# Two chained two-layer blocks on one core: conv entry of the second layer and both attention entries, in another order of work

## The chip, the cores and the metric

One core of one Trainium2 chip runs the whole program. The metric is device time in microseconds (us) of that core, the median of several runs. TensorE (PE in the rows), VectorE (DVE), ScalarE (ACT), GpSimd (POOL) and SyncE (SP, here only a DMA queue and its waits) each run an instruction stream that was written out by hand, and they meet only at semaphores.

## What is computed

Two different blocks of two layers each, on a sequence of 512 tokens with 1024 channels. Everything below happens in the first block, in which a layer is:

```
ml = ada_mod(c, w_ada[l], b_ada[l], 6); mc = ada_mod(c_ctx, ...)
zl = modulate(x, ml[0], ml[1]) @ w_in[l] + b_in[l]          # 512 tokens
q, k, v = qkv_heads(zl); context k, v from ctx (256 tokens) # 8 query heads, 2 key heads
attn = softmax(q @ k_all.T * scale) @ v_all                 # 768 keys
conv = silu(layer_norm(depthwise_conv(a * sigmoid(gt), 31 taps))) @ conv_pw_w
pool = multiscale_pool(...) @ pool_w
x = layer_norm(ALPHA * x + ml[2] * ((g0*attn + g1*conv + g2*pool) @ w_out))
x = layer_norm(ALPHA * x + ml[5] * conv_ffn(modulate(x, ml[3], ml[4])))
```

The first layer (l = 0) treats 768 tokens, latent and context together, the second (l = 1) 512 tokens, and of the context only keys and values. Between the layers a small projection for the second block ("ple") is computed early and stored.

## The kernel before

**Weights.** A unit is a 128x1024 block of fp32 weights, the columns for one output tile of 128 channels. SyncE loads it into one of two raw buffers (w_raw, by the parity of the unit), ScalarE rounds it into w_hi (weight_hi, L1398), VectorE or GpSimd subtracts to get w_lo (L2188 on VectorE in the conv stages, L550 on GpSimd in the attention and behind it). w_hi and w_lo have four slots. A product takes 24 matmuls for a unit: w_hi with act_hi, w_lo with act_hi, w_hi with act_lo, eight chunks each. ScalarE "refills" a slot (refill) after it has taken the result of the unit that used it, and SyncE loads a raw buffer when the subtraction that read it is done. So unit 7 can't be loaded before unit 5 is split, and SyncE's list is in order: a wait in it holds all loads behind it.

**Conv entry of the second layer.** The stage "conv" has 16 units: even ones give the values, odd ones the gates. Units 0 to 3 run together (first_four, L633), so that TensorE can follow the input chunk by chunk. Then single units (L684) follow. ScalarE takes an even unit with Identity (L1590), an odd one with Sigmoid (L1593), each followed by a refill. Behind the first of them stand the two copies of the "ple" projection out of PSUM tiles 3 and 2 (L1599) and the DMA that stores it (L1602). VectorE multiplies a pair to a chunk (glu, L2388), subtracts a weight half, does some taps of the 31-tap depthwise convolution (conv_taps: a tap is one instruction, L2411 or L2419 in turn; a chunk ends with an addition L2425 and begins with a copy L2401), subtracts the next half, and so on. Ahead of certain units TensorE does a step of the modulation matrices (ada_ahead, ada_step, L872), whose weights SyncE loads between the units and only once an earlier step has freed their buffer. ADA_AT says ahead of which unit stands which step. Step 24 is the first one that sums into PSUM tile 2, so it waits until the second "ple" copy has left that tile:

```python
                    if h == 24:
                        pe.wait_ge(tile_free[2], taken(l, "ada_rest", 2, 0))
```

**Attention.** The 32 tiles of 128 queries go in order (attention, three functions of this name for TensorE, ScalarE and VectorE). For tile it: TensorE makes the scores (s_tile, L987 or L993), VectorE the maximum (L2362, L2364), ScalarE exp (L1519), VectorE the normalization (L2369, L2371), TensorE the transposes (t_tile, L788), ScalarE copies them out (L1529), TensorE multiplies with the values (pair, L800). TensorE's order is scores of it + 2, transposes of it, half a pair. Scores of it + 2 wait for exp of it, transposes for the normalization. VectorE's order is normalization of it, maximum of it + 2, conv taps (more_taps: per_tile, 1 in the first layer, 2 in the second). Before the first tile ScalarE takes the value tiles (L1654) in two copies. In the second layer it then makes the w_hi of two units (L1398), which GpSimd splits, and loads the table for exp (L1673). TAPS_AT holds how many taps stand where, its last number those in front of the merge of the third gate (at_first_unit).

## Time and profile before

| | |
|---|---|
| median of 3 runs | 3144.55 us (3144.37 to 3147.13) |
| profiled execution: time, span | 3145.95 us, 3144.2 us |
| TensorE busy | 3064.6 us, 97% |
| VectorE, ScalarE, GpSimd busy | 63%, 37%, 26% |
| conv stage of the second layer, by the trace | about 1456.9 to 1563 us |
| attention of first and second layer | about 374 to 483 and 1697 to 1817 us |

A row of a timeline has the start (us from the start of the span), the duration, the engine, the line of the kernel, the operation, what it writes and reads, the shape and how many instructions of one form were merged. In brackets stands how long the engine had been idle before it and what ended that. The chain shows which engine's work led to the end: TensorE's has 89% of it.

### The profile page before, as it was taken

To read this page: it belongs to the slowest core of one execution; us is meant where nothing else is said; L and a number is where in the kernel's file an instruction comes from. 1 tells how busy PE (TensorE), PEld (TensorE's weight loads), DVE (VectorE), ACT (ScalarE), POOL (GpSimd) and SP (SyncE) were. 2 spreads that over 40 slices of the span, in tenths; PEclk is the share of its full clock that TensorE was granted. 3 is DMA by queue.
4 is the path that set the end of the run, shared out by engine and by line. 5 is a ranking of instruction groups with operands and counts; after the bars stand their busy time and mean duration, and the time that the engine had idled before them with its cause. 6 is when DMAs were issued, how large, how long until landed. Compare 5 with 4: busy or idle time off the path is not lost.

```text
span 3144.2 us, 43692 instructions
## 1 busy us (share of the span) xinstructions
PE 3064.6 (97%) x16056; PEld 2598.6 (83%) x16056; DVE 1979.9 (63%) x2784; ACT 1152.7 (37%) x1661; POOL 806.7 (26%) x330
## 2 busy tenths in 40 slices
PE   7999999999999999999999999999999999999998
PEld 5999887899999999997777677778887686777766
DVE  5899987644576164356989985664646466445443
ACT  3122364233243221224334535443223535443443
POOL 0001212233323232231012024511545332233312
PEclk8999999999999999999999999999999999999999
DMA  7442001112212212123541022423233212122212
GB/s 289 175 171 82 28 1 65 45 59 101 81 61 67 73 60 67 61 67 136 193 163 55 1 67 87 144 80 101 94 95 108 75 59 79 54 78 77 78 60 67
DMA packets 77709, 275.25 MB, mean 88 GB/s; under 512 B 8688, under 2 KB 11888, under 8 KB 76656
## 3 DMA queue, kind: packets, MB, share of 16 engines
q1 hardware_dynamic: 70800, 253.94, 24.3%
q10 hardware_dynamic: 6752, 19.14, 1.7%
q8 instruction: 108, 1.77, 0.2%
q14 instruction: 49, 0.40, 0.0%
HBM read 266.75 MB, written 6.29 MB: 87 GB/s over the span
## 4 chain that ended last, share of the span: by engine, by line
PE 89%; DVE 5%; ACT 2%; issue 1%; DVEq 1%; DMA 0%; SPq 0%; ACTq 0%
PE ps L684 53%; PE ps L1065 11%; PE ps L619 5%; PE ps L633 2%; PE ps L800 2%; PE ps L1210 1%; PE ps L872 1%; PE ps L963 1%; PE ps L788 1%; PE ps L993 1%; PE ps L1289 1%; DVE small L2362 1%; PE ps L691 1%; PE ps L1307 1%; PE ps L1016 1%
## 5 line engine op out<-in xcount | busy, mean ns | idle before, releaser
L550 POOL TENSOR_TENSOR w_lo<-w_raw,w_hi 128x1024 fp32r<-128x1024 f32 x308 | 789.8, 2568 | 2195.9 <-ACT w_hi L1398 2195.9
L1398 ACT ACTIVATE w_hi<-w_raw 128x1024 fp32r<-128x1024 f32 x376 | 395.8, 1056 | 561.5 <-PE ps L684 286.6
L684 PE MATMUL ps<-act_hi,w_hi 128*128 128x384 f32 (+1 forms) x2544 | 529.8, 356 | 4.4 <-DVE w_lo L2188 2.5
L684 PE MATMUL ps<-act_hi,w_lo 128*128 128x384 f32 (+1 forms) x2544 | 519.4, 352 | 0.0
L684 PE MATMUL ps<-act_lo,w_hi 128*128 128x384 f32 (+1 forms) x2544 | 519.2, 352 | 0.0
L684 PEld LDWEIGHTS ps<-act_hi,w_hi 128*128 128x128 f32 x2544 | 451.0, 188 | 70.5 <-issue 34.7
L684 PEld LDWEIGHTS ps<-act_hi,w_lo 128*128 128x128 f32 x2544 | 455.0, 188 | 32.4
L684 PEld LDWEIGHTS ps<-act_lo,w_hi 128*128 128x128 f32 x2544 | 454.3, 188 | 32.3 <-issue 0.5
L2256 DVE SCALAR_TENSOR_TENSOR x<-ps,mod,x 128x384 f32<-128x384 f32 (+1 forms) x128 | 64.2, 546 | 277.3 <-PE ps L684 222.7
L2419 DVE SCALAR_TENSOR_TENSOR x<-arena,vec,x 128x512 f32<-128x512 f32 x336 | 228.2, 706 | 0.0
L2411 DVE SCALAR_TENSOR_TENSOR arena<-arena,vec 128x783 f32<-128x783 f32 (+1 forms) x240 | 226.2, 943 | 0.0
L2658 DVE SCALAR_TENSOR_TENSOR arena<-arena,vec 128x769 f32<-128x769 f32 (+1 forms) x88 | 145.9, 1658 | 15.4 <-issue 15.4
L1471 ACT ACTIVATE arena<-ps,vec 128x768 f32<-128x768 f32 (+3 forms) x64 | 50.8, 794 | 277.4 <-PE ps L684 206.7
L1065 PE MATMUL ps<-act_hi,w_hi 128*128 128x512 f32 x432 | 117.5, 403 | 1.9 <-ACT vec L1440 0.8
L1065 PE MATMUL ps<-act_lo,w_hi 128*128 128x512 f32 x432 | 111.7, 390 | 1.5 <-DVE act_lo L2734 1.5
L1065 PE MATMUL ps<-act_hi,w_lo 128*128 128x512 f32 x432 | 111.5, 390 | 0.0
L2655 DVE TENSOR_SCALAR arena<-arena,vec 128x769 f32<-128x769 f32 (+1 forms) x44 | 29.1, 661 | 125.7 <-ACT arena L1796 125.7
L1796 ACT ACTIVATE arena<-ps 128x384 f32<-128x384 f32 (+3 forms) x88 | 33.8, 440 | 202.1 <-PE ps L684 197.1
L800 PE MATMUL ps<-arena 128*128 128x256 f32 x416 | 103.1, 381 | 2.6 <-ACT arena L1663 2.5
L2162 DVE TENSOR_TENSOR ffn_lo<-arena,ffn_hi 128x768 f32 (+1 forms) x44 | 101.1, 2298 | 6.5
L1065 PEld LDWEIGHTS ps<-act_hi,w_hi 128*128 128x128 f32 x432 | 78.7, 188 | 28.2 <-issue 12.1
L1065 PEld LDWEIGHTS ps<-act_lo,w_hi 128*128 128x128 f32 x432 | 80.8, 188 | 19.9 <-DVE act_lo L2734 3.3
(380 smaller groups left out, 4551.8 us busy)
## 6 DMA issues: line engine op xcount, KB each, us to landing
w_raw<-in_weights SPq DMA_DIRECT2D x376, 512.0 KB, 3.4
arena<-in_ada_w SPq DMA_DIRECT2D x75, 512.0 KB, 4.8
tmp<-in_ada_w SPq DMA_DIRECT2D x21, 512.0 KB, 6.3
x<-in_x SPq DMA_DIRECT2D x2, 1536.0 KB, 19.2
x<-in_x ACTq DMA_DIRECT2D x1, 3072.0 KB, 10.5
arena<-in_pool_w ACTq DMA_DIRECT2D x2, 1024.0 KB, 4.8
x_mid<-x ACTq DMA_DIRECT2D x1, 2048.0 KB, 7.1
x<-x_mid ACTq DMA_DIRECT2D x1, 2048.0 KB, 8.4
```

Of the source, the lines that this page charges most:

```text
L550: nc.gpsimd.tensor_tensor(WL[:, w], raw, WH[:, w].bitcast(f32), ALU.subtract).then_inc(units_split, 1)
L619: last = nc.tensor.matmul(ps(tb + s, o, o + b - a), w[:, s * UNIT + k * P:s * UNIT + (k + 1) * P], act[:, k * TOK + a:k * TOK + b], start= ...
L633: last = nc.tensor.matmul(tile(0, s, o, o + b - a), w[:, s * UNIT + k * P:s * UNIT + (k + 1) * P], act[:, k * TOK + a:k * TOK + b], start= ...
L684: last = nc.tensor.matmul(tile(o, o + b - a), w[:, s * UNIT + k * P:s * UNIT + (k + 1) * P], act[:, k * TOK + a:k * TOK + b], start=(n == ...
L800: last = nc.tensor.matmul(ps(3, (m % 2) * 512, (m % 2) * 512 + 2 * P), values(m, k), AR[:, a:a + 2 * P], start=(k == 0), stop=(k == nk - 1))
L1065: return nc.tensor.matmul(out, w0[:, k0:k0 + P], act[:, k * n:k * n + SEQ], start=start, stop=stop)
L1398: nc.scalar.activation(WH[:, s * UNIT:(s + 1) * UNIT], RAW[:, (s % 2) * UNIT:(s % 2 + 1) * UNIT], ACT.Copy).then_inc(hi_done, 1)
L2162: return V.tensor_tensor(lo, src, hi.bitcast(f32), ALU.subtract)
L2256: last = V.scalar_tensor_tensor(x, ps(t, o, o + b - a), at(MOD, mod(l, gate, j, m), 1), x, ALU.mult, ALU.add)
L2411: t = V.scalar_tensor_tensor(acc, src, w, acc, ALU.mult, ALU.add)
L2419: t = V.scalar_tensor_tensor(acc, src, w, acc, ALU.mult, ALU.add)
L2658: t = V.scalar_tensor_tensor(cv, src, w, cv, ALU.mult, ALU.add)
```

## The change

It moves work and adds or removes none, apart from where taps of the convolution are done. (1) Second layer, conv entry: the two "ple" copies and their store stand behind ScalarE's fourth unit and no longer behind its first. (2) The modulation steps 24 to 31 stand ahead of units 5, 7, 9, 11, 13, 15, 16, 17 instead of 3, 5, ..., 17. (3) Both attention entries: the table for exp is loaded ahead of the copies of the value tiles. (4) Second layer: the two weight halves that ScalarE made there come behind tiles 4 and 8. (5) Both layers: one tap stands behind the first two maxima, none behind tiles 0 and 1, one behind tile 2, then as before. In the second layer that leaves 60 taps in the attention where there were 64, and at_first_unit is 16 for 12.

```diff
-           (9, 7, 8, (2, 2, 2, 2, 2, 2, 1, 1, 0, 0), 2, (2, 2, 2, 2), 12))
+           (9, 7, 8, (2, 2, 2, 2, 2, 2, 1, 1, 0, 0), 2, (2, 2, 2, 2), 16))
-          {**{2 * i + 3: (24 + i,) for i in range(CH)}, **{u: (14 + u,) for u in range(18, 24)}, 24: (38, 39)})
+          {**{u: (24 + i,) for i, u in enumerate((5, 7, 9, 11, 13, 15, 16, 17))}, **{u: (14 + u,) for u in range(18, 24)}, 24: (38, 39)})
@@ ScalarE, conv
                     refill(l, "conv", i, s)
-                    if l and u == 0:
+                    if l and u == SLOTS - 1:
                         act.wait_ge(ple_mm, 3)
@@ ScalarE, attention entry
+                nc.scalar.preload_act_table_set("natural_log_exp_and_others")
                 for s, n in enumerate((1024, 512)):
...
-                if l not in HALVED:
-                    for s in (2, 3):
-                        refill(l, "qkv", 2, s)
-
...
-                nc.scalar.preload_act_table_set("natural_log_exp_and_others")
+                def next_weights(it):
+                    if it in (4, 8):
+                        refill(l, "qkv", 2, 1 + it // 4)
+
                 act.drain()
-                heads("attn", 0, 4, 6, next_query if l in HALVED else None)
+                heads("attn", 0, 4, 6, next_query if l in HALVED else next_weights)
@@ VectorE, attention
                 maximum(0)
                 maximum(1)
+                if also:
+                    also(2)
@@ VectorE, block1
                 def more_taps(it):
                     nonlocal done
-                    done = conv_taps(l, done, per_tile[it % 4])
+                    done = conv_taps(l, done, per_tile[it % 4] if it > 2 else int(it == 2))
```

TensorE at the conv entry, from the end of unit 3 on, before. The L684 rows are single units (unit 4, then the start of unit 5), the L872 rows the steps 24 (the first two) and 25 (the other three).

```order
L872 MATMUL ps<-arena,gla_w 32x512 [waits ada_landed1,ada_landed0,tile_free2]
L872 MATMUL ps<-arena,gla_w 32x512 x3
L684 MATMUL ps<-act_hi,w_hi 128x512 [waits tile_free0,units_split]
L684 MATMUL ps<-act_hi,w_hi 128x512 x7
L684 MATMUL ps<-act_hi,w_lo 128x512 x8
L684 MATMUL ps<-act_lo,w_hi 128x512 x8
L872 MATMUL ps<-arena,gla_w 32x512 [waits ada_landed3,ada_landed2]
L872 MATMUL ps<-arena,gla_w 32x512
L872 MATMUL ps<-tmp,gla_w 32x512 x2
L684 MATMUL ps<-act_hi,w_hi 128x512 [waits tile_free1,units_split]
L684 MATMUL ps<-act_hi,w_hi 128x512 x7
L684 MATMUL ps<-act_hi,w_lo 128x512 x8
```

And of the change, the same place:

```order
L684 MATMUL ps<-act_hi,w_hi 128x512 [waits tile_free0,units_split]
L684 MATMUL ps<-act_hi,w_hi 128x512 x7
L684 MATMUL ps<-act_hi,w_lo 128x512 x8
L684 MATMUL ps<-act_lo,w_hi 128x512 x8
L872 MATMUL ps<-arena,gla_w 32x512 [waits ada_landed1,ada_landed0,tile_free2]
L872 MATMUL ps<-arena,gla_w 32x512 x3
L684 MATMUL ps<-act_hi,w_hi 128x512 [waits tile_free1,units_split]
L684 MATMUL ps<-act_hi,w_hi 128x512 x7
L684 MATMUL ps<-act_hi,w_lo 128x512 x8
L684 MATMUL ps<-act_lo,w_hi 128x512 x8
L684 MATMUL ps<-act_hi,w_hi 128x512 [waits tile_free0,units_split]
```

Step 24, with its wait for tile_free2, has moved from ahead of unit 4 to behind it, and step 25 is gone from here (it stands ahead of unit 7).

ScalarE at the same place, from the taking of unit 0, before:

```order
L1590 ACTIVATE arena<-ps,vec 128x512 [waits units_used]
L1398 ACTIVATE w_hi<-w_raw 128x1024 [waits raw_landed0,units_used]
L1599 ACTIVATE ple_proj_early<-ps 128x1024 [waits ple_projected]
L1599 ACTIVATE ple_proj_early<-ps 128x512
L1602 DMA pp_mid<-ple_proj_early 128x1536 [waits tile_free2,tile_free3]
L1593 ACT_TABLE_LOAD
L1593 ACTIVATE arena<-ps,vec 128x512 [waits units_used]
L1398 ACTIVATE w_hi<-w_raw 128x1024 [waits raw_landed1,units_used]
```

And of the change:

```order
L1590 ACTIVATE arena<-ps,vec 128x512 [waits units_used]
L1398 ACTIVATE w_hi<-w_raw 128x1024 [waits raw_landed0,units_used]
L1593 ACT_TABLE_LOAD
L1593 ACTIVATE arena<-ps,vec 128x512 [waits units_used]
L1398 ACTIVATE w_hi<-w_raw 128x1024 [waits raw_landed1,units_used]
L1590 ACTIVATE arena<-ps,vec 128x512 [waits units_used]
L1398 ACTIVATE w_hi<-w_raw 128x1024 [waits raw_landed0,units_used]
L1593 ACTIVATE arena<-ps,vec 128x512 [waits units_used]
L1398 ACTIVATE w_hi<-w_raw 128x1024 [waits raw_landed1,units_used]
L1599 ACTIVATE ple_proj_early<-ps 128x1024 [waits ple_projected]
L1599 ACTIVATE ple_proj_early<-ps 128x512
L1602 DMA pp_mid<-ple_proj_early 128x1536 [waits tile_free2,tile_free3]
```

The two L1599 copies, which free tiles 3 and 2, and the L1602 store now stand behind the w_hi of units 5, 6 and 7 (L1398 with raw_landed1, raw_landed0, raw_landed1).

ScalarE at the second layer's attention entry, from the root of the query norms (L1645) to the first exps (L1519), before:

```order
L1645 ACTIVATE arena<-ps,cst 128x32 [waits block0_norm_ms]
L1654 ACTIVATE arena<-ps 128x4x256 [waits block0_v_mm]
L1654 ACTIVATE arena<-ps 128x2x256 [waits units_used]
L1398 ACTIVATE w_hi<-w_raw 128x1024 [waits raw_landed0,units_used]
L1398 ACTIVATE w_hi<-w_raw 128x1024 [waits raw_landed1,units_used]
L1673 ACT_TABLE_LOAD
L1519 ACTIVATE tmp,small<-ps,small,arena 128x768 [waits block0_attn_max] x2
```

And of the change (the copies of the value tiles have the line 1655 there):

```order
L1645 ACTIVATE arena<-ps,cst 128x32 [waits block0_norm_ms]
L1648 ACT_TABLE_LOAD
L1655 ACTIVATE arena<-ps 128x4x256 [waits block0_v_mm]
L1655 ACTIVATE arena<-ps 128x2x256 [waits units_used]
L1519 ACTIVATE tmp,small<-ps,small,arena 128x768 [waits block0_attn_max] x2
```

The table load went ahead of the copies, and the two w_hi (L1398) are gone from here. They stand behind the exps of tiles 6 and 10.

VectorE there, from the second maximum on, before (L2411 and L2419 are taps, L2371 is the normalization of a tile):

```order
L2364 TENSOR_SCALAR small<-small,arena 128x1
L2369 RECIPROCAL small<-small 128x1
L2371 TENSOR_SCALAR tmp<-tmp,small 128x768
L2362 TENSOR_REDUCE small<-ps 128x1
L2364 TENSOR_SCALAR small<-small,arena 128x1
L2411 SCALAR_TENSOR_TENSOR arena<-arena,vec 128x512
L2419 SCALAR_TENSOR_TENSOR x<-arena,vec,x 128x512
L2369 RECIPROCAL small<-small 128x1
L2371 TENSOR_SCALAR tmp<-tmp,small 128x768
L2362 TENSOR_REDUCE small<-ps 128x1
```

And of the change (its taps have the lines 2413 and 2421):

```order
L2364 TENSOR_SCALAR small<-small,arena 128x1
L2413 SCALAR_TENSOR_TENSOR arena<-arena,vec 128x512
L2369 RECIPROCAL small<-small 128x1
L2371 TENSOR_SCALAR tmp<-tmp,small 128x768
L2362 TENSOR_REDUCE small<-ps 128x1
L2364 TENSOR_SCALAR small<-small,arena 128x1
L2369 RECIPROCAL small<-small 128x1
L2371 TENSOR_SCALAR tmp<-tmp,small 128x768
L2362 TENSOR_REDUCE small<-ps 128x1
L2364 TENSOR_SCALAR small<-small,arena 128x1
```

One tap came in front of the first normalization, and those behind the first two tiles are gone.

## Rows read from the trace of the kernel before

**Rows 1.** The page, busy time of the engines.

```profile
PE 3064.6 (97%) x16056; PEld 2598.6 (83%) x16056; DVE 1979.9 (63%) x2784; ACT 1152.7 (37%) x1661; POOL 806.7 (26%) x330
```

**Rows 2.** Stretches: start:end, length, busy time by engine, PEclk, DMA share, GB/s.

```profile
1482.40:1489.70 7.30, 7.29 (x24) 5.57 (x24) 7.18 (x12) 1.64 (x2) 0.00 (x0) 0.77 0.67 231
1489.70:1570.00 80.30, 80.30 (x381) 60.32 (x384) 76.41 (x117) 27.87 (x37) 0.00 (x0) 1.00 0.57 195
1697.00:1713.00 16.00, 9.52 (x41) 5.46 (x40) 11.94 (x23) 9.39 (x14) 4.64 (x2) 1.00 0.22 66
374.00:387.00 13.00, 9.25 (x56) 7.57 (x55) 10.65 (x21) 9.02 (x15) 0.73 (x1) 1.00 0.00 1
```

**Rows 3.** Timeline of TensorE, conv entry of the second layer.

```profile
1478.89 1.06 PE L872 MATMUL ps<-arena,gla_w 128*32 128x512 f32 x8
1482.41 2.86 PE L684 MATMUL ps<-act_hi,w_hi 128*128 128x512 f32 x8 [2.45 <-DVE w_lo L2188]
...
1490.72 2.12 PE L684 MATMUL ps<-act_hi,w_hi 128*128 128x512 f32 x8
...
1502.82 2.12 PE L684 MATMUL ps<-act_hi,w_hi 128*128 128x512 f32 x8
```

**Rows 4.** Timeline of ScalarE, same place.

```profile
1475.51 1.05 ACT L1398 ACTIVATE w_hi<-w_raw 128x1024 fp32r<-128x1024 f32 x1
1476.46 1.50 ACT L1599 ACTIVATE ple_proj_early<-ps 128x1024 f32<-128x1024 f32 x2
...
1478.41 1.28 ACT L1593 ACT_TABLE_LOAD   x1 [0.45 <-ACT ple_proj_early L1599]
1479.71 0.69 ACT L1593 ACTIVATE arena<-ps,vec 128x512 f32<-128x512 f32 x1
...
1490.28 1.06 ACT L1398 ACTIVATE w_hi<-w_raw 128x1024 fp32r<-128x1024 f32 x1 [2.33 <-DMA w_raw<-in_weights]
```

**Rows 5.** Timeline of VectorE, same place.

```profile
1479.28 0.74 DVE L2498 MEMSET arena<- 128x814 f32 x1 [6.95 <-DMA x_mid<-arena]
...
1481.14 1.22 DVE L2188 TENSOR_TENSOR w_lo<-w_raw,w_hi 128x1024 fp32r<-128x1024 f32 x1
```

**Rows 6.** Timeline of SyncE, same place, the load of unit 7.

```profile
1486.53 0.33 SPq L480 DMA_DIRECT2D w_raw<-in_weights  x1
```

**Rows 7.** Timeline of ScalarE, attention entry of the second layer.

```profile
1698.31 1.99 ACT L1398 ACTIVATE w_hi<-w_raw 128x1024 fp32r<-128x1024 f32 x2
...
1701.68 0.99 ACT L1519 ACTIVATE tmp<-ps,small,arena 128x768 f32<-128x768 f32 x1
```

**Rows 8.** Timeline of GpSimd and VectorE, same place.

```profile
1699.53 4.64 POOL L550 TENSOR_TENSOR w_lo<-w_raw,w_hi 128x1024 fp32r<-128x1024 f32 x2 [15.42 <-ACT w_hi L1398]
...
1700.14 0.21 DVE L2364 TENSOR_SCALAR small<-small,arena 128x1 f32<-128x1 f32 x1
...
1703.03 1.56 DVE L2371 TENSOR_SCALAR tmp<-tmp,small 128x768 f32<-128x768 f32 x1
...
1706.04 0.74 DVE L2411 SCALAR_TENSOR_TENSOR arena<-arena,vec 128x512 f32<-128x512 f32 x1
...
1707.60 0.62 DVE L2371 TENSOR_SCALAR tmp<-tmp,small 128x768 f32<-128x768 f32 x1
```

**Rows 9.** Timeline of TensorE, transposes of tiles 2 and 4, second layer.

```profile
1712.73 0.88 PE L788 MATMUL ps<-ident,tmp 128*128 128x128 f32 x6 [2.29 <-DVE tmp L2371]
...
1719.63 0.87 PE L788 MATMUL ps<-ident,tmp 128*128 128x128 f32 x6 [0.19 <-DVE tmp L2371]
```

**Rows 10.** Timeline of VectorE and TensorE, third gate of the second layer.

```profile
1884.32 2.89 DVE L2411 SCALAR_TENSOR_TENSOR arena<-arena,vec 128x512 f32<-128x512 f32 x1
...
1915.34 0.69 DVE L2425 TENSOR_TENSOR x<-x,arena 128x512 f32<-128x512 f32 x1
...
1918.72 0.64 PE L699 MATMUL ps<-x,ones_in_one_column 128*32 128x512 f32 x4
```

**Rows 11.** Timeline of ScalarE, attention entry of the first layer, the first exp.

```profile
376.50 0.99 ACT L1519 ACTIVATE tmp<-ps,small,arena 128x768 f32<-128x768 f32 x1 [0.45 <-DVE small L2364]
```

## The prediction

> **What bounds the kernel now.** I read the page's busy times first: TensorE works in 97% of the span [rows 1]. So only two things count, stretches in which TensorE idles and stretches in which it runs at a low clock. The stretches by engine show where they are [rows 2]. At the second layer's conv entry TensorE idles 2.45 us ahead of unit 4, until VectorE's w_lo is there [rows 3], and over unit 4 its mean granted clock is 0.77. From 1489.70 to 1570.00 it is busy in all of 80.30 us at clock 1.00 [rows 2]. What delays it in the conv stage is therefore not made good behind it. At the second layer's attention entry it idles 16.00 - 9.52 = 6.48 us between 1697 and 1713, at the first layer's 13.00 - 9.25 = 3.75 us between 374 and 387 [rows 2]. In the tiles that follow it waits 0.19 us for VectorE in the 6.90 us of two tiles [rows 9]: VectorE and TensorE are nearly level there, so a delay of VectorE shows in TensorE.
>
> The sum is made against the profiled execution, 3145.95 us; the median of the runs, 3144.55, lies 1.4 below, and I take that off at the end. A change of 0.2%, 6.3 us, is about what a measurement of this kernel can tell from none.
>
> **Conv entry: what is gained.** Unit 4 waits for w_lo, 1481.14 + 1.22 [rows 5]. Ahead of that on VectorE stands the product of the first pair, which needs the first Sigmoid, 1479.71 + 0.69, and that came behind the two "ple" copies (1.50), 0.45 of idle and the table load (1.28) [rows 4]. With the copies gone the load starts at about 1476.56, behind w_hi of unit 4 (1475.51 + 1.05), and the Sigmoid is done about 1478.6. But VectorE is held by another thing too: its memset waits for the transfer of x_mid and ends at 1479.28 + 0.74 = 1480.02 [rows 5], and the product can't start before it, where it now starts at about 1480.5 (w_lo's start less a product of some 0.6). Unit 4 starts at about 1481.85, **0.55 earlier**. This only counts through what follows.
>
> **Conv entry: what is paid.** Step 24 must wait until the second copy has left PSUM tile 2. Before, it took 1.06 us ahead of unit 4 [rows 3], inside a time in which TensorE would have waited anyway: free of charge. Now it stands behind unit 4, while the copies stand behind the w_hi of units 6 and 7. These wait for their weights from DRAM: w_hi of unit 7 waited 2.33 us for its load and started at 1490.28 [rows 4]; the load had been issued at 1486.53 [rows 6], once unit 5 was split. That whole chain moves with the entry, so 1490.28 - 0.55 + 1.06 = 1490.8, then the copies, 1.50: tile 2 is free at about 1492.2 (1492.3 by the terms; a little of the second instruction overlaps). Step 24, some 1.0, then unit 5 at about 1493.2, where it started at 1490.72 [rows 3]. **+2.5**, with the 0.55 of the entry already in it. Unit 4 will be done long before, at 1487 to 1489, so TensorE idles 3 to 5 us at step 24.
>
> One step more: between units 5 and 17 TensorE did the steps 26 to 31 (six) and one of them will be a seventh, since step 24 no longer sits in a gap, step 25 stands ahead of unit 7, and the last is ahead of unit 17 as before. **+1.1**, a step of 1.06.
>
> The clock: before, units 5 and 6 with one step took 1502.82 - 1490.72 = 12.10 us [rows 3], so a unit at full clock is (12.10 - 1.06) / 2 = 5.52. Unit 4 with step 25 took 1490.72 - 1482.41 = 8.31, less the step 7.25: 1.73 lost to the clock of 0.77 in that stretch [rows 2], behind an idle time of 2.45. That loss stands in both kernels. Idle time of 3 to 5 us ahead of step 24 is longer than that one, and the likeliest is that unit 5 pays as unit 4 did. **+1.7** (0 if the clock holds).
>
> SyncE's list: the load of the weights for a later modulation step waits for step 24 and stands ahead of the load of unit 8. That load goes out some 2 us later than before, with over 10 us until the unit is used, so 0; if that cover were gone, it would cost those 2.
>
> Conv entry: 2.5 + 1.1 + 1.7 = **+5.3**.
>
> **Attention entry, second layer.** The first exp starts at 1701.68, behind 1.99 us of w_hi and a table load [rows 7], though its maximum was done at 1700.14 + 0.21 = 1700.35 [rows 8]. Without both it starts at about 1700.4: 1.3 earlier. VectorE's first normalization took 1.56 us while GpSimd's two w_lo ran (4.64 us, [rows 8]); alone one takes 0.62 (the last row there), so 0.94 is regained. The taps behind tiles 0 and 1 (0.74 each, [rows 8]) go out of VectorE's path to tiles 1 and 2: at least three of them stood there. 1.3 + 0.9 + 3 to 4 x 0.74 = 4.4 to 5.2, and TensorE's idle time of 6.48 covers all of it. I take **-5.2** at the transposes of tile 2 (1712.73 [rows 9]).
>
> Then it is partly given back, since VectorE is nearly level. The change of chunk in the convolution (an addition and a copy, about 0.7 each) comes at tile 3 now, where no idle time is left: **+1.3**. The two w_lo on GpSimd, 4.64 / 2 = 2.32 each, come behind tiles 4 and 8. A VectorE tap that fell beside such work took 2.89 instead of 0.74 [rows 10], 2.15 longer; the normalization above lost 0.94. Each w_lo thus costs VectorE between 0.94 and 2.15, of which the idle 0.19 per pair of tiles hides little. I take the middle, 1.5: **+3.0**. The Trainium skill (SBUF — State Buffer, SBUF: two separate sides) says that VectorE and GpSimd share a port under an exclusive lock for a whole instruction, so the loser stands for all of it. The 2.89 of the tap agrees. By that rule the two would cost 2 x 2.3 = 4.6, an estimate, and the whole would come 1.6 higher. Net of this entry: -5.2 + 1.3 + 3.0 = **-0.9**.
>
> **Attention entry, first layer.** The first exp waits 0.45 us for VectorE's maximum [rows 11], so the table load was hidden already: 0. One tap goes in front of the first normalization, where VectorE waits for exp, and two groups of three leave the path to tiles 1 and 2, all inside 3.75 us of idle time [rows 2]; what ends it soonest is then ScalarE's exps of 0.99 us [rows 11], one of which is on the way twice. I take **-1.2**; the bounds are 0 and -3.75. The taps that are left over go to stages with several us of slack: 0.
>
> The Trainium skill (ScalarE: Activation LUTs, What ACT_TABLE_LOAD costs) puts a switch at 1283 ns and a drain of about 1380 behind it. Row and rule agree on the load (1.28); the next activation stood 1.30 behind the load's start [rows 4], so no drain shows. By the page 1.4 more would be regained at the second attention entry, and the whole come to +2.8.
>
> **Third gate, second layer.** Four taps more stand ahead of the last addition of the convolution, which ended at 1915.34 + 0.69 = 1916.03; TensorE takes that chunk in the fifth of its sums, which begin at 1918.72, four matmuls in 0.64 [rows 10]. 4 x 0.7, less about 0.6 of idle time, gives 1918.2, and up to 1920.9 if one of GpSimd's instructions, which cost a tap there 2.89 [rows 10], falls in. Needed at about 1919.7: between 0 and 1.2, or 2.3 with more behind it. I take **+1.0**.
>
> **Sum.** +5.3 - 0.9 - 1.2 + 1.0 = +4.2: 3150.15 by the profiled execution, **3148.8** by the median, 0.13% slower and so inside what counts as no change.
>
> **Rivals.**
> *The steps' wait doesn't bite* (the other side). If units 6 and 7 are landed sooner than I read, the copies are done before unit 4 ends. That decides at about 1487.3, 4.9 us ahead of my time, and rows 4 speak against it: w_hi of unit 7 waits for its load. TensorE then has no second idle time, and if the shorter first one (1.9) keeps the clock, unit 4 gains 1.73: -0.55 - 1.73 + 1.1 = -1.2 in the conv stage, all together -1.2 - 0.9 - 1.2 + 1.0 = -2.3: 3142.3. It needs every lesser loss to be small too. A chance of 0.15.
> *The clock holds* at step 24: 4.2 - 1.7 = +2.5, 3147.1. For it speaks that matmuls run right up to the idle time; against it, the 2.45 us before unit 4 were enough. 0.14.
> *A heavier one.* Each w_lo holds VectorE for 2.15 (+1.3), and TensorE's low clock reaches one stretch further (+1.7): +7.2, 3151.8. The row of 2.89 speaks for the first; for the second, that the idle time is the longer one. 0.13.
> *My forecast*: 0.58, its own range 3146.0 to 3151.0.
>
> **How the numbers follow.** The range goes from 3142.8 (a little above the first rival) to 3152.6 (above the heavier one, with the third gate's other 1.3 in part); it leaves out about 2 in 10, half below and half above. The limits of 0.2% are 3138.3 and 3150.8. Faster than the lower one would need the first rival and the whole 3.75 at the first layer's entry: 0.05. Slower than the upper one: most of the heavier case (0.09) and the upper end of my forecast (0.07): 0.16. Within: 0.79.
>
> **What the profile of the changed kernel would show.** Step 24 (L872) behind unit 4 with 3 to 5 us of idle time that ScalarE's "ple" copy ends, unit 5 at about 1493, and a granted clock under 1 behind it; a normalization or tap of near 2.9 us at about tiles 5 and 9 or a little behind; the first exp of the second layer at about the entry's 1700.4 (moved by what the conv stage lost), the idle time ahead of tile 2's transposes gone, about 1.2 us less of it in the first layer; an idle time of about 1 us ahead of L699 in the third gate. The prediction is wrong if step 24 finds tile 2 free, if w_lo beside the tiles costs VectorE nothing, or if later waits, which TensorE's slack now hides, come out when the attention entry no longer holds it.

## The result, and the profile after

| | before | changed |
|---|---|---|
| first timing, median of 11 runs | 3146.13 us (3144.03 to 3149.56) | 3152.12 us (3150.57 to 3154.09) |
| ratio | | 1.0022, interval 1.0014 to 1.0030 |
| second timing, medians of 13 and 9 runs | 3144.87 us | 3152.51 us |
| ratio | | 1.0026, interval 1.0016 to 1.0036 |
| profiled execution: time, span | 3145.95 us, 3144.2 us | 3151.19 us, 3149.4 us |

By the medians the change makes the kernel slower by 6.0 us in the first timing and by 7.6 us in the second; by the ratios, whose intervals leave out 1, it is 0.22 and 0.26%. Forecast was 4.2 us, 0.13%, and a chance of 0.79 for a difference too small to be told from none. It was told, so the likeliest case was not the one that came. The time itself, 3152.12 us, lies just below the upper end of the range, 3152.6.

The busy times of the changed kernel's page, beside [rows 1]:

```profile
PE 3067.0 (97%) x16056; PEld 2600.3 (83%) x16056; DVE 1983.8 (63%) x2784; ACT 1152.8 (37%) x1661; POOL 805.1 (26%) x330
```

TensorE does the same 16056 matmuls in 2.4 us more busy time. That is a low clock, not work; the other 2.8 us of the longer span (3149.4 for 3144.2) are idle time. At the conv entry, the timeline of TensorE, beside [rows 3]:

```profile
1481.75 3.56 PE L684 MATMUL ps<-act_hi,w_hi 128*128 128x512 f32 x8 [2.83 <-DVE w_lo L2188]
1485.11 2.17 PE L684 MATMUL ps<-act_hi,w_lo 128*128 128x512 f32 x8
1487.12 1.98 PE L684 MATMUL ps<-act_lo,w_hi 128*128 128x512 f32 x8
1491.92 1.65 PE L872 MATMUL ps<-arena,gla_w 128*32 128x512 f32 x8 [2.82 <-ACT ple_proj_early L1599]
1493.51 3.10 PE L684 MATMUL ps<-act_hi,w_hi 128*128 128x512 f32 x8
1496.45 2.00 PE L684 MATMUL ps<-act_hi,w_lo 128*128 128x512 f32 x8
```

Unit 4 starts 0.66 us earlier than before. Step 24 then waits 2.82 us for the "ple" copy, and unit 5 starts at 1493.51. The first eight matmuls of a unit, which take 2.12 us at full clock [rows 3], take 3.56 behind the first idle time and 3.10 behind the second, and step 24 takes 1.65 for 1.06: the clock is at its lower level of 1.2 GHz for part of both (mean granted clock 0.76 from 1481.75 to 1489.00 and 0.79 from 1491.92 to 1500.00; 1.00 from there to 1570.00). What the step waits for is seen in the chain of work of the changed kernel over this stretch (start, us, what):

```profile
1484.56 1.14 DVE w_lo L2188
...
1485.72 0.05 SPq L480
...
1485.87 3.41 DMA w_raw<-in_weights
...
1489.41 1.06 ACT w_hi L1398
1490.47 1.41 ACT ple_proj_early L1599 x2
...
1491.92 1.65 PE ps L872 x8
```

It is read from top to bottom: the split of unit 5 lets SyncE load unit 7, the load takes 3.41 us, ScalarE rounds it, and only then makes the copies. TensorE's step hangs on a DMA that it has nothing to do with.

The whole kernel can be cut at rows that stand in both traces. These are TensorE's rows at the ends of three stages before (first layer's attention, conv stage, part of the second block):

```profile
373.95 0.51 PE L987 MATMUL ps<-w_hi 128*128 128x512 f32 x2
...
508.97 1.23 PE L684 MATMUL ps<-act_hi,w_hi 128*128 128x384 f32 x5
...
1478.58 0.39 PE L633 MATMUL ps<-act_lo,w_hi 128*128 128x512 f32 x1
...
1568.94 0.95 PE L882 MATMUL ps<-ident,arena 128*128 128x8 f32 x8
...
2430.67 1.06 PE L749 MATMUL ps<-arena,ones_in_one_column 128*32 128x512 f32 x8
...
2729.74 1.07 PE L1048 MATMUL ps<-arena,ones_in_one_column 128*32 128x512 f32 x8
```

And all the cuts for the changed kernel:

```profile
373.06 0.51 PE L987 MATMUL ps<-w_hi 128*128 128x512 f32 x2
...
508.92 1.40 PE L684 MATMUL ps<-act_hi,w_hi 128*128 128x384 f32 x6
...
1478.53 0.39 PE L633 MATMUL ps<-act_lo,w_hi 128*128 128x512 f32 x1
...
1573.97 0.95 PE L882 MATMUL ps<-ident,arena 128*128 128x8 f32 x8
...
1702.64 1.89 PE L993 MATMUL ps<-arena 128*128 128x512 f32 x5
...
1815.82 0.88 PE L788 MATMUL ps<-ident,tmp 128*128 128x128 f32 x6
...
1930.70 1.02 PE L691 MATMUL ps<-arena,ones 128*128 128x512 f32 x2
...
2435.15 1.07 PE L749 MATMUL ps<-arena,ones_in_one_column 128*32 128x512 f32 x8
...
2735.86 1.06 PE L1048 MATMUL ps<-arena,ones_in_one_column 128*32 128x512 f32 x8
```

The length of a stage is the difference of two starts. Both kernels were profiled four times, and a stage has the same length within 0.1 us each time:

| stage, from which start to which | before, 4 profiles | changed, 4 profiles | difference | forecast |
|---|---|---|---|---|
| attention of the first layer (L987 to L684) | 135.02 to 135.13 | 135.80 to 135.86 | +0.8 | -1.2 |
| conv stage of the second layer (L633 to L882) | 90.33 to 90.36 | 95.41 to 95.49 | +5.1 | +5.3 |
| attention of the second layer (L993 to L788) | 114.31 to 114.34 | 113.18 to 113.20 | -1.1 | -0.9 |
| up to behind the third gate (L788 to L691) | 114.18 to 114.24 | 114.87 to 114.88 | +0.7 | +1.0 |
| part of the second block (L749 to L1048) | 299.04 to 299.08 | 300.71 to 300.76 | +1.7 | none |
| sum | | | +7.1 | +4.2 |

The stages between these are the same within 0.2 us. The start of the program, up to the first of these rows, varies from profile to profile by 0.5 us in before and 1.4 in the changed kernel, and its end by 0.9 in before. The whole spans of the four profiles average 3143.4 us before and 3149.8 changed, 6.4 apart.

The fifth row is in a stage that the change doesn't touch. First before, then the changed kernel, TensorE's timeline in the second block's attention:

```profile
2691.14 0.66 PE L1324 MATMUL ps<-ident,tmp 128*128 128x128 f32 x4 [1.30 <-DVE tmp L2945]
2692.58 0.63 PE L1324 MATMUL ps<-ident,tmp 128*128 128x128 f32 x4 [0.78 <-ACT arena L2062]
2693.04 3.62 PE L1336 MATMUL ps<-arena 128*128 128x256 f32 x16
```

```profile
2695.59 0.66 PE L1324 MATMUL ps<-ident,tmp 128*128 128x128 f32 x4 [1.31 <-DVE tmp L2947]
2697.03 0.97 PE L1324 MATMUL ps<-ident,tmp 128*128 128x128 f32 x4 [0.78 <-ACT arena L2062]
2697.79 5.00 PE L1336 MATMUL ps<-arena 128*128 128x256 f32 x16
```

The idle times ahead are equal, 1.30 and 1.31, then 0.78 and 0.78. Behind them four transposes take 0.63 us in the one and 0.97 in the other, and the same sixteen matmuls 3.62 and 5.00: 1.7 us in all. By the stretches, the mean granted clock from 2690 to 2715 is 1.00 before and 0.93 after.

### The profile page after: what moved, and what is told of

It reads as the page before. It is cut to its first block, busy times and chain, and to the rows that moved or that the text cites. A ratio compares the mean times of both kernels' runs of the same rounds, so it can differ in the third digit from the quotient of the medians.

```text
span 3149.4 us, 43691 instructions
## 1 busy us (share of the span) xinstructions
PE 3067.0 (97%) x16056; PEld 2600.3 (83%) x16056; DVE 1983.8 (63%) x2784; ACT 1152.8 (37%) x1661; POOL 805.1 (26%) x330
## 3 DMA queue, kind: packets, MB, share of 16 engines
q8 instruction: 108, 1.77, 0.2%
## 4 chain that ended last, share of the span: by engine, by line
PE 87%; DVE 7%; ACT 2%; issue 2%; DVEq 1%; DMA 1%; SPq 0%; ACTq 0%; POOL 0%
PE ps L684 52%; PE ps L1065 11%; PE ps L619 4%; PE ps L800 2%; PE ps L633 2%; PE ps L1210 1%; PE ps L872 1%; PE ps L963 1%; PE ps L788 1%; PE ps L993 1%; PE ps L1289 1%; DVE small L2362 1%; PE ps L691 1%; DVE arena L2413 1%; PE ps L1307 1%
## 5 line engine op out<-in xcount | busy, mean ns | idle before, releaser
L1398 ACT ACTIVATE w_hi<-w_raw 128x1024 fp32r<-128x1024 f32 x376 | 395.9, 1056 | 593.7 <-PE ps L684 294.6
L684 PE MATMUL ps<-act_hi,w_hi 128*128 128x384 f32 (+1 forms) x2544 | 531.6, 357 | 4.7 <-DVE w_lo L2188 2.8
L684 PE MATMUL ps<-act_lo,w_hi 128*128 128x384 f32 (+1 forms) x2544 | 519.2, 352 | 0.0
L684 PE MATMUL ps<-act_hi,w_lo 128*128 128x384 f32 (+1 forms) x2544 | 518.6, 352 | 0.0
L684 PEld LDWEIGHTS ps<-act_hi,w_hi 128*128 128x128 f32 x2544 | 452.3, 188 | 72.1 <-issue 37.8
L684 PEld LDWEIGHTS ps<-act_hi,w_lo 128*128 128x128 f32 x2544 | 454.5, 188 | 32.2
L684 PEld LDWEIGHTS ps<-act_lo,w_hi 128*128 128x128 f32 x2544 | 454.3, 188 | 32.3 <-issue 0.5
L2421 DVE SCALAR_TENSOR_TENSOR x<-arena,vec,x 128x512 f32<-128x512 f32 x336 | 237.3, 734 | 0.0
```

The lines of the kernel that those rows point to most:

```text
L684: last = nc.tensor.matmul(tile(o, o + b - a), w[:, s * UNIT + k * P:s * UNIT + (k + 1) * P], act[:, k * TOK + a:k * TOK + b], start=(n == ...
L1398: nc.scalar.activation(WH[:, s * UNIT:(s + 1) * UNIT], RAW[:, (s % 2) * UNIT:(s % 2 + 1) * UNIT], ACT.Copy).then_inc(hi_done, 1)
L2421: t = V.scalar_tensor_tensor(acc, src, w, acc, ALU.mult, ALU.add)
```

## The experiments

Each is an edit of before or of the changed kernel. Times are medians beside before on the same chip; what a stage gained or lost is cut from the profile as above. That profile is one execution: it is the slowest of its kernel's runs for x2, x4 and x9, for x7 too but for a single one of 5445 us, and the fastest for x3 and x5, so what its stages add up to can lie 1 to 3 us from the median.

**The conv part alone** (before, with these two edits of the change):

```diff
-          {**{2 * i + 3: (24 + i,) for i in range(CH)}, ...
+          {**{u: (24 + i,) for i, u in enumerate((5, 7, 9, 11, 13, 15, 16, 17))}, ...
-                    if l and u == 0:
+                    if l and u == SLOTS - 1:
```

> The conv entry part of the change alone: copies behind ScalarE's fourth unit, steps 24 to 31 ahead of units 5 to 17; attention and taps as before. Theory A (step 24 waits for the late copies, TensorE idles and its clock falls, and a step that was free of charge now lies on its path): the whole loss of the conv stage comes with this part: unit 5 starts about 2.8 us later than before, the stage ends about 5.0 later, and nothing of it is made good behind it: 5.0 us slower in all, 0.16%. Theory B (the attention entries and the taps cost the time): under 1 us slower. Theory C (the two profiled executions differ by chance in the conv stage): unit 5 within 1 us of before.

3150.84 us against 3144.58, ratio 1.0020 (1.0011 to 1.0029). Conv stage 95.43 for 90.34, +5.1, unit 5 at 1494.57; no other stage of the table differs. Theory A holds, B and C fall: the conv part is the loss. The median is 1.2 us more than the stage; in the profile the first layer's attention starts at 374.55, 0.6 to 1.1 later than in the four of before, ahead of everything that was edited.

**The steps alone** (only the first of those two edits):

> Only the steps 24 to 31 moved to units 5 to 17; the copies stay behind ScalarE's first unit. Theory A: the copies are long done when step 24 comes, so no second idle time and no second low clock. Only the step that used to lie in the gap ahead of unit 4 is paid: unit 5 starts at the same time as before (within 0.3), from unit 17 on everything is 1.1 us later, 1.1 slower in all. Theory D (the new places of the steps, with their weights' loads in SyncE's order, cost the time, and where the copies stand doesn't matter): 4 to 5 us slower, as with the whole conv part.

3148.22 us, 3.6 more than before, ratio 1.0010 (1.0001 to 1.0019). The conv stage is 91.55, +1.2, as Theory A had it. But the whole isn't 1.1: the second attention is 1.0 longer, though nothing in it was edited. The other 1.0 of this profile lies ahead of the first row, where it starts at 374.92 for 373.95 and nothing was edited either; its end is as long as in the first profile of before (414.4 us). TensorE at the attention entry of this kernel:

```profile
1704.97 2.64 PE L993 MATMUL ps<-arena 128*128 128x512 f32 x4 [2.45 <-ACT tmp L1519]
1707.41 1.46 PE L788 MATMUL ps<-ident,tmp 128*128 128x128 f32 x6
```

Before, the same four matmuls took 1.56 us behind the same 2.45 of idle time and the six transposes 0.87. So the clock can be low in a stage in which nothing was edited.

**The change, with the copies behind unit 1:**

```diff
-                    if l and u == SLOTS - 1:
+                    if l and u == 1:
```

> The whole change with one edit: the two copies and their store stand behind ScalarE's second unit and no longer behind its fourth. The table load stays early. Theory A: w_hi of unit 6 waits over 4 us for its load there, so the copies cost ScalarE nothing and end by about 1482; step 24 finds its tile free behind unit 4. The 2.8 us of idle time and the low clock at unit 5 go: conv stage about +0.5 against before (-0.6 from the early table load, +1.1 for the step), with the attention's -1.2 and the third gate's +0.65 the whole comes to 0.0, 5 us less than the change. Theory D: 4 us slower than before still.

3146.18 us, 1.6 over before, ratio 1.0005 (0.9996 to 1.0015), some 5 less than the change. The conv stage is 90.88, +0.5: the second idle time is gone, step 24 stands right behind unit 4 (1489.40), unit 5 starts at 1490.39. Theory D falls: the loads are in the order of the change here. The stages sum up to +0.8, since the first layer's attention is 0.8 longer here too; the 0.0 expected had left that out.

**The attention parts alone** (the change without its conv part):

> Everything but the conv entry part: table load, weight halves and taps as in the change. Theory A: the second attention entry gives 1.2 us and the third gate takes 0.65 back, the first layer's entry gives nothing in the end: 0.5 us faster, within 0.3% of nothing. Theory B: it is this part that is 4 to 5 us slower.

3143.90 us against 3144.58, ratio 0.9998 (0.9989 to 1.0007). First attention +0.8, second -1.15, third gate +0.65: Theory B falls. The first layer's +0.8 was not expected; with it the stages sum up to +0.3, where 0.5 us faster was expected, and the median is 0.7 faster, inside the noise.

**Weight halves back at the entry** (before with the table load and the taps of the change):

> Conv entry as before; table load and taps as in the change, but the two weight halves stay at the attention entry. Theory A: the two GpSimd subtractions no longer hold a VectorE tap in the loop, so the two idle times of about 1.5 us ahead of the transposes go (2.6 us back). In the entry they now hold the first tap and the first normalization until about 1704, so the gain at tile 2 is about 3.5 us and not 5.3. The attention ends about 2.0 us earlier than before, the third gate takes 0.65: 1.3 us faster in all, where the entry part as in the change gave 0.5. Rival: the locks cost the entry as much as the loop, 0.5 us faster or less.

3145.21 us against 3144.97, ratio 1.0001 (0.9992 to 1.0010). The second attention is 112.54, -1.8 (expected -2.0), and 0.65 shorter than with the halves moved: where VectorE stands while GpSimd subtracts (called a lock here), it costs more in the loop than at the entry. The whole gained nothing that can be measured. The profiled execution (3142.5 us) is the fastest of its 11, and in it unit 4 ran at full clock behind 2.45 us of idle time, with the conv stage at 88.72; the median of its runs is 2.7 us longer. Whether unit 4 runs at full clock in those too isn't shown. The same profile has a low clock in the first layer's attention, at 378, where no other run has it, and that stage is 136.38 us long.

**Weight halves moved alone:**

> Only the weight halves moved behind tiles 4 and 8. Theory A: the first normalization is no longer held (1.56 us falls to 0.62) and comes after a first exp at about 1700.4: 2.1 us gained in the entry; two taps of about 2.06 us in the loop take 2.6 back: 0.5 us slower in all. Rival (a lock in the loop is hidden by TensorE's lead): 2 us faster.

3147.85 us against 3144.97, ratio 1.0010 (1.0001 to 1.0019). The second attention is 1.3 longer (expected 0.5; the entry gave 1.4 at the transposes of tile 2, not 2.1), and the second block's stage is 1.7 longer by the low clock at 2693. The rival, 2 us faster, falls.

**The copies ahead of unit 1's refill, steps as before:**

```diff
-                    refill(l, "conv", i, s)
-                    if l and u == 0:
+                    if l and u == 1:
                         act.wait_ge(ple_mm, 3)
...
                         act.dma_start(pp_mid[:, 2048:3584], ...
+                    refill(l, "conv", i, s)
```

> Conv entry alone, in another order: the two copies stand behind ScalarE's first Sigmoid, ahead of w_hi of unit 5; the steps stay where they were before (24 ahead of unit 4). The table load and the Sigmoid come 1.5 us earlier, step 24 waits for the copies until about 1480.5 and still lies in the gap. Theory A: unit 4 starts at about 1481.85, 0.5 earlier, and the step stays free of charge: 0.5 us faster. Where the idle time, now in two pieces of 1.7 and 0.3 us, leaves the clock up, unit 4 gains another 1.7: 2.3 us faster. Theory D (it is the order of the loads that matters): no difference to before.

3144.39 us against 3144.97, ratio 0.9997 (0.9989 to 1.0006). The conv stage is 88.08, -2.3: 0.5 by the earlier start, 1.7 by the clock. The second attention, untouched, took that back: 116.73, +2.4, with low clock at 1702 and again at 1714. The first layer's attention, untouched too and ahead of the edit, took 136.25, +1.2, with low clock at 488.

**Before again, three more profiles:**

> The kernel before, once more, timed against itself and profiled a second time. A ratio of 1.000 within 0.0003; its profile shows whether unit 4 and the second attention entry run at the same clock in every execution. If unit 4 is not always slow here, the moved steps (whose longer idle time makes it slow each time) cost more than two single profiles show.

> The kernel before, profiled once more. Counted is whether unit 4 (idle time of 2.45 us ahead of it) and the scores at 1702 (2.45 too) run slow. Theory E (the clock's fall behind an idle time is a matter of chance, the likelier the longer the idle time): unit 4 is slow in some executions of before and in all of the kernels with the steps moved. Rival: unit 4 is slow in every execution of before, and the full speed seen in one other kernel was due to that kernel.

> The kernel before, profiled a fourth time, to count how often unit 4 runs slow behind its 2.45 us of idle time. Theory E: in some executions, not in all. Rival: in all.

Timed against itself: 3144.67 against 3144.97, ratio 1.0000 (0.9991 to 1.0009). Unit 4 is slow in all four profiles, the scores at 1702 in none, so for this kernel the rival to Theory E holds in all four: nothing here speaks for chance from one execution to the next.

**The copies behind unit 1, a second profile:**

> The change with the copies behind unit 1, profiled a second time. Theory E: unit 4, behind 2.8 us of idle time in one piece, is slow again; the rest of the conv stage as in the first profile (+0.4 against before). Rival: it runs at full clock as often as in before.

3147.79 us, 2.2 more than in its first profile. Conv stage 90.89 again, unit 4 slow again. The rest of the 2.2 and more lies in two places that ran slow here and not in the first profile: sixteen matmuls at 3031 (L1336, 5.30 us for 3.62) and the last ones of the program at 3134 (L1058, 2.08 for 1.12). For this kernel the clock does differ between two executions.

**The change again:**

> The changed kernel again, beside before on one chip. By the stages of the trace it is 4.5 us slower (conv +5.0, attention -1.2, third gate +0.65); the two medians of 11 runs said 6.0. Theory E: what is left over is low clock in stages that the change doesn't touch, in which some executions are slow and some not; this profile then has the same 4.5 at the same stages and other slow places. The ratio again 1.0015 to 1.0022.

> The changed kernel, profiled a third time. Theory E: units 4 and 5 slow again, conv stage +5.0 within 0.2; at the attention entry (about 1706) and at about 2697 slow in some of the profiles only. Rival (a wait outside the conv and attention stages that the change adds): the same further loss in all profiles at one place.

> The changed kernel, profiled a fourth time, for the same count: units 4 and 5 slow again, conv stage +5.0 within 0.2, other slow places (about 1706, 2697, 3137) in some profiles only.

3152.51 us against 3144.87, ratio 1.0026. The stages are those of the table. The slow stretch at 2697 is in all four profiles of the changed kernel and in none of before. Theory E, which had it come and go, is wrong in this; and the rival, a wait, is wrong too: no idle time differs there, only the clock.

**The steps alone, a second profile:**

> Only the steps moved, profiled a second time. Theory E: conv stage +1.2 again, unit 4 slow again behind 3.45 us of idle time; the second attention entry, slow in the first profile (+1.0), at full clock here or not, by chance. Rival: slow there again, since the moved steps change something there.

3148.82 us. Conv stage 91.52, second attention 115.30: slow at 1704.72 again, as the rival said.

**The gains together:**

> The parts that gained, together: copies behind the first Sigmoid and ahead of w_hi of unit 5, steps as before, table load and taps as in the change, weight halves at the second attention entry. Without chance in the clock: conv entry -0.55, attention -1.8, third gate +0.6, so 1.75 us faster than before; with unit 4 at full clock more often than before, up to 3.5 faster (0.06 to 0.11%, at the edge of what can be measured).

3143.10 us against 3145.14, ratio 0.9994 (0.9985 to 1.0003). Conv -1.95, second attention -0.5 (low clock at its entry), third gate +0.65, first attention +0.8, second block +1.7 (low clock at 2692): +0.7 in the profiled execution, the slowest of its 11, where the median is 2.0 us faster than before.

**The first layer's taps undone in the change:**

```diff
-                if also:
+                if also and l:
                     also(2)
...
-                    done = conv_taps(l, done, per_tile[it % 4] if it > 2 else int(it == 2))
+                    done = conv_taps(l, done, per_tile[it % 4] if it > 2 or l == 0 else int(it == 2))
```

> The change with its taps undone in the first layer alone. From the start of that layer's scores to its output projection before took 135.02 us and the change 135.84 in every profile; the theory that the moved taps do this (a longer wait for GpSimd in the entry, a normalization held by GpSimd later) says 135.0 here, and 0.8 us less in all than the change: about 6.0 slower than before, if the low clock at about 2697 stays. Rival (the table load, moved too, does it): 135.8 still.

3151.24 us against 3144.85, ratio 1.0020 (1.0011 to 1.0029). The first attention is 135.04: the taps make the 0.8, the table load nothing. All other stages are those of the change, the slow stretch of the second block too.

**The gains, without the first layer's taps:**

> The best parts (copies behind the first Sigmoid and ahead of the second refill, steps as before, table load early, weight halves at the entry), with the second layer's taps as in the change and the first layer's as before. From the stages: conv entry -2.3 with unit 4 at full clock, second attention -1.8, third gate +0.65: 3.4 us faster; a low clock at 1705 or at 2692, as in x9, would take 1.1 and 1.7 of it back. By the profile 0.8 less than x9 in the first layer's attention.

3141.59 us against 3144.85, ratio 0.9989 (0.9980 to 0.9998): 3.3 us faster than before, 0.10%, the fastest version here. Its stages: 135.02, 88.15, 112.55, 114.84 and 299.10, so -2.2 in the conv stage, -1.8 in the second attention, +0.65 at the third gate. TensorE at its conv entry:

```profile
1480.17 1.06 PE L872 MATMUL ps<-arena,gla_w 128*32 128x512 f32 x8 [1.05 <-ACT ple_proj_early L1598]
1481.96 2.14 PE L684 MATMUL ps<-act_hi,w_hi 128*128 128x512 f32 x8 [0.72 <-DVE w_lo L2188]
```

Step 24 cuts the idle time in two pieces of 1.05 and 0.72 us, and unit 4 runs at full clock. The pieces are also less in sum, 1.77 us for 2.45; no run tells the cut from the lesser sum.

## Why the prediction was wrong

**The conv entry was right.** Step 24 waits for the copies behind the load of unit 7, as the prediction had it: unit 5 at 1493.51 (1493.2 forecast), the stage +5.1 (+5.3), the clock low at unit 5 too, the step no longer free (x2: +1.2 for a term of 1.1). The terms are right too: from the stage's start unit 5 comes 2.8 us later, of which 0.6 is step 24 at low clock, so 2.2 for the term of 2.5; and the clock costs 0.6 there and 1.0 in unit 5, 1.6 for 1.7. The rival in which the wait doesn't bite fell in all profiles. The idle time ahead of the step was 2.82 us, just under the 3 to 5 that I gave.

**The second attention entry was right, with its parts.** These are TensorE's transposes of the changed kernel, beside [rows 9]:

```profile
1712.44 0.88 PE L788 MATMUL ps<-ident,tmp 128*128 128x128 f32 x6
...
1720.54 0.87 PE L788 MATMUL ps<-ident,tmp 128*128 128x128 f32 x6 [1.39 <-DVE tmp L2371]
...
1728.76 0.87 PE L788 MATMUL ps<-ident,tmp 128*128 128x128 f32 x6 [1.51 <-DVE tmp L2371]
...
1743.86 0.88 PE L788 MATMUL ps<-ident,tmp 128*128 128x128 f32 x6 [1.49 <-DVE tmp L2371]
```

From the first scores, the transposes of tile 2 stand at 1712.44 - 1702.64 = 9.80, before at 1712.73 - 1697.62 = 15.11: -5.3, for a term of -5.2. Then come the change of chunk (1.39 for 0.19, +1.2; forecast +1.3) and the two locks (1.51 and 1.49 for 0.19, +1.3 each; forecast +1.5). That leaves -1.5 at tile 10; about 0.4 more is lost where the next chunk changes (at tile 19 behind 0.87 us of idle time, before at tile 17 behind 0.51), which the sum did not have. GpSimd and VectorE at the first of them:

```profile
1724.36 2.36 POOL L550 TENSOR_TENSOR w_lo<-w_raw,w_hi 128x1024 fp32r<-128x1024 f32 x1 [35.21 <-ACT w_hi L1398]
...
1725.21 2.06 DVE L2421 SCALAR_TENSOR_TENSOR x<-arena,vec,x 128x512 f32<-128x512 f32 x1
```

The subtraction ends at 1726.72 and the tap, which takes 0.74 us alone, 0.55 later: it stands until the other is nearly done, and loses 1.3 because it came 0.85 late. By the Trainium skill (SBUF — State Buffer, SBUF: two separate sides), of a GpSimd instruction and a VectorE instruction with two inputs in SBUF, as a tap is, the one that starts first has the shared port for its whole length and the other stands. The trace agrees, 2.06 us for a tap of 0.74. What I had as "by that rule", 2.3 each, took the tap to arrive at the first moment of the subtraction.

The table load was right without a drain: in the changed kernel it stands in ScalarE's idle time ahead of the value copies, and the copy follows 0.02 us behind its end:

```profile
1697.31 1.28 ACT L1648 ACT_TABLE_LOAD   x1
1698.61 1.03 ACT L1655 ACTIVATE arena<-ps 128x1024 f32<-128x1024 f32 x1
...
1705.42 0.99 ACT L1519 ACTIVATE tmp<-ps,small,arena 128x768 f32<-128x768 f32 x1 [1.98 <-DVE small L2364]
```

The first exp waits for its maximum there, and starts 2.78 us behind the first scores where it was 4.06, 1.3 earlier as forecast. The 1.4 us more that would have been given back by the Trainium skill (ScalarE: Activation LUTs, What ACT_TABLE_LOAD costs) did not come.

**The third gate was right but for its size**, +0.7 for +1.0. Between its sums TensorE now waits for the convolution's last addition, which before was done in time [rows 10]. One tap beside a GpSimd subtraction, 2.89 us at 1919.78, falls in as the upper bound had it:

```profile
1922.58 1.07 PE L699 MATMUL ps<-x,ones_in_one_column 128*32 128x512 f32 x8
...
1923.37 0.69 DVE L2427 TENSOR_TENSOR x<-x,arena 128x512 f32<-128x512 f32 x1
...
1924.12 1.06 PE L699 MATMUL ps<-x,ones_in_one_column 128*32 128x512 f32 x8 [0.47 <-DVE x L2427]
```

**Where it failed, first: "I take -1.2"** for the first layer's attention, with bounds of 0 and -3.75. It measured +0.8, outside them. The taps did leave the path to tiles 1 and 2, but two other waits came out. First, the timeline of TensorE at the scores of tile 4, before and then in the changed kernel. They are the first that need queries whose halves are made within the loop:

```profile
382.68 0.59 PE L987 MATMUL ps<-w_hi 128*128 128x512 f32 x2
```

```profile
382.44 0.59 PE L987 MATMUL ps<-w_hi 128*128 128x512 f32 x2 [1.15 <-POOL w_lo L565]
```

Second, VectorE, GpSimd and TensorE at the transposes of tile 9, first the rows of VectorE and TensorE before, then the changed kernel:

```profile
406.37 0.62 DVE L2371 TENSOR_SCALAR tmp<-tmp,small 128x768 f32<-128x768 f32 x1
...
407.22 0.82 PE L788 MATMUL ps<-ident,tmp 128*128 128x128 f32 x6
```

```profile
405.78 1.15 DVE L2371 TENSOR_SCALAR tmp<-tmp,small 128x768 f32<-128x768 f32 x1 [0.43 <-issue]
405.79 0.73 POOL L565 TENSOR_TENSOR w_lo<-arena,w_hi 128x256 fp32r<-128x256 f32 x1 [5.56 <-ACT w_hi L1510]
...
406.99 0.88 PE L788 MATMUL ps<-ident,tmp 128*128 128x128 f32 x6 [1.05 <-DVE tmp L2371]
```

TensorE now waits 1.15 us for GpSimd's low half of the queries, which was ready in time before, so the entry gives 0.5 us (transposes of tile 2 at 10.52 from the first scores for 11.04) and not 1.2. And in the level loop such a GpSimd subtraction now starts within 0.01 us of a normalization, which takes 1.15 us for 0.62; TensorE idles 1.05 there, where it otherwise idles 0.17, and the transposes of tile 9 come 0.7 late (33.93 for 33.27). Before had an idle time of the same length, 1.07, at tile 21, where the changed kernel has 0.74 at tile 22: there the two are level again, and the 0.8 in which they end comes in the last ten tiles, a little at a time (102.19 for 101.34 at tile 30, behind idle times of 1.22 and 0.76). What lengthens those last waits was not looked into. Summed over the timeline from 374 to 484, TensorE's idle times (the numbers in brackets) are 8.3 us before and 9.1 after. I had worked the giving back out for the second layer (chunk change, locks) and left it out for the first, where VectorE is as level (0.17 us of waiting in two tiles). That is the error: a gain at the entry of a loop in which two engines are level must be followed to the loop's end. x17, which undoes only these taps, takes the 0.8 away.

**Where it failed, second: the sum has no term for the clock outside the conv stage.** The signs of being wrong at its end name later waits, not this. TensorE loses 1.7 us at 2697 behind idle times that before has too, in each of four profiles. Together the two are 2.0 + 1.7 = 3.7 us; the other terms were 0.8 too high in all (5.3 - 0.9 + 1.0 = 5.4 forecast, 5.10 - 1.13 + 0.66 = 4.6 measured), and 4.2 + 3.7 - 0.8 = 7.1. Without the clock's 1.7 the change would cost 5.4 us. The heavier case, at 3151.8 with a chance of 0.13, had the size, but by other means: "one stretch further" of low clock in the conv stage, which no profile shows, and 2.15 for each weight half, which measured 1.3.

The median of three runs to which the forecast was set, 3144.55, was not far off: before gave 3146.13 beside the first timing of the change and 3144.58 to 3145.14 in the five later timings.

**What stays open.** What decides behind which idle time the clock falls was not found; no run sets it by itself. It is mostly the same for one kernel: before slow at unit 4 in four profiles and at 2692 in none, the change slow at 2697 in four, the steps alone slow at 1704 in two; but the kernel with the copies behind unit 1 was slow at 3031 and 3134 in one profile of two. It is not the same for two kernels with equal idle times at the place, and it isn't the kernel's delay at that place alone: x6 is slow there when it comes 0.43 us later than in the first profile of before, x4 at 0.39 is not. The stages of the kernel with the copies behind unit 1 sum up to +0.8 in its first profile, and the second is 2.2 us longer; its median is 1.6 over before. So single profiles can be off by more than what is looked for here.

## What to carry to other kernels

A copy that frees a PSUM tile belongs ahead of any instruction of its engine that waits for a load: behind one, the tile's next user hangs on DRAM (the change and x3, whose conv stages are 4.5 us apart). Small work that sits in an idle time of the bounding engine is free; moving it out cost 1.2 us for the step. Put in the middle of it, it also splits it: unit 4 ran at full clock in the three kernels that did so (x7, x9, x18), and at low clock in before, where the step stood at the beginning. Where two engines are level in a loop, work out a gain at its entry to the end of the loop, with each collision at its new phase; and where a difference is under 0.3%, cut both traces into stages and profile more than once before giving a cause to the rest.

## What was not expected of the hardware

A fall of TensorE's clock cost 1.6 to 1.7 us where it lay fully inside matmuls (conv stage 90.3 us against 88.7 in x5, second block 300.7 against 299.1), and less where part of it fell in idle time (1.0 in x2's second attention). Behind 2.45 us of idle time, unit 4 was slow in six profiles of seven (four of before, x4, x6, not x5); behind 2.8 to 3.5 us in one piece in all ten profiles of kernels with the steps moved; behind two pieces of 1.05 and 0.7 us (x7, x9 and x18) in none of three. At the second attention entry 2.45 us of idle time were followed by full clock in five profiles (four of before, x1) and by a low one in three (x2 twice, x7). And it fell at 2692 to 2697 behind idle times of 1.3 and 0.8 us, in the four profiles of the change, x17, x6 and x9, and in none of the others. So an edit early in the program can go with a loss of 1.7 us a thousand microseconds later, in work that it doesn't touch; what carries it there isn't shown.
